# The first five rotations wholly on VectorE, one value tile back between indexer blocks, an earlier sum of squares and odd modulations on VectorE

## What is computed

```
ada = silu(c) @ w_ada + b_ada                     # shifts, scales, gates
h = rms_norm(x, g_pre_mix) * (1 + sc1) + sh1      # modulated input
qa, ka, va, qi, ki, wi, qb, kb, vb, ga, gb = split(h @ w_in)
qa, ka, qi, ki, qb, kb = rope(...)                # rotary positions
score = sum over 8 heads of wi * relu(qi . ki)    # indexer, masked; top-k keys per query
oa = attention(qa, ka, va) over the top-k keys
ob = differential attention(qb, kb, vb)
m = sigmoid(ga) * (oa @ w_o_a) + sigmoid(gb) * (ob @ w_o_b)
x = x + gate * rms_norm(m @ w_out)
x = x + gate * rms_norm(swiglu(modulated rms_norm(x)))
```

## Time and profile before

| | us |
|---|---|
| median of 3 runs (1062.88 to 1063.39) | 1063.2 |
| the profiled execution's own time | 1065.39 |
| its span, first to last instruction | 1063.5 |
| PE busy in the span | 970.6 |
| DVE / ACT / POOL busy | 397.4 / 403.1 / 384.8 |

### The profile page before, as it was taken

One profiled execution on the slowest core, in us unless ns is written; L12 is line 12 of the kernel. 1 busy time (PEld: TensorE's weight loads), 2 busy tenths in 40 slices (PEclk: granted clock), 3 DMA queues, 4 the chain that ended last, 5 costly groups with the idle time before them and its releaser, 6 DMA issues.

```text
span 1063.5 us, 17552 instructions
## 1 busy us (share of the span) xinstructions
PE 970.6 (91%) x7100; PEld 920.0 (87%) x7100; DVE 397.4 (37%) x734; ACT 403.1 (38%) x723; POOL 384.8 (36%) x194
## 2 busy tenths in 40 slices
PE   4789797999999989989999659999999999999995
PEld 1677797999988989878888449999999999999995
DVE  3566884876764333143200552222222221000005
ACT  3654223656555455343333362222222222322221
POOL 2443016466263231224544203333333332444440
PEclk9899898999999999989999889999999999999998
DMA  9631012222222013247865102222222221222212
GB/s 369 251 118 45 1 56 96 99 96 71 102 93 71 21 43 131 72 156 259 319 214 193 39 1 82 87 89 79 79 79 80 90 86 54 83 82 83 82 56 90
DMA packets 33663, 111.58 MB, mean 105 GB/s; under 512 B 4224, under 2 KB 7296, under 8 KB 33216
## 3 DMA queue, kind: packets, MB, share of 16 engines
q1 hardware_dynamic: 29216, 102.48, 27.6%
q10 hardware_dynamic: 4112, 6.93, 1.7%
q0 software_dynamic: 272, 1.31, 0.3%
HBM read 100.38 MB, written 10.32 MB: 104 GB/s over the span
## 4 chain that ended last, share of the span: by engine, by line
PE 77%; issue 8%; ACT 5%; DVE 5%; POOL 2%; DMA 1%; SPq 0%; ACTq 0%; DVEq 0%; POOLq 0%
PE pj L1502 53%; PE pj L1714 12%; PE pvb L1624 3%; PE lg L1474 2%; PE tb L1608 2%; PE pj L1687 1%; DMA raw<-in_w_ada 1%; PE lg L1737 1%; PE lg L1739 1%; PE lg L1738 1%; PE pj L1493 1%; DVE ro L536 1%; ACT hf L961 1%; POOL zc L1056 1%; ACT whi L707 1%
## 5 line engine op out<-in xcount | busy, mean ns | idle before, releaser
L1502 PE MATMUL pj<-hh,whi 128*128 128x288 f32 x1248 | 279.2, 306 | 23.4 <-DVE hl L1189 15.5
L1502 PE MATMUL pj<-hl,whi 128*128 128x288 f32 x1248 | 269.9, 298 | 0.0
L1502 PE MATMUL pj<-hh,wlo 128*128 128x288 f32 x1248 | 269.7, 298 | 0.0
L1502 PEld LDWEIGHTS pj<-hh,whi 128*128 128x128 f32 x1248 | 202.6, 192 | 29.2 <-issue 19.1
L1502 PEld LDWEIGHTS pj<-hl,whi 128*128 128x128 f32 x1248 | 204.0, 192 | 0.0
L1502 PEld LDWEIGHTS pj<-hh,wlo 128*128 128x128 f32 x1248 | 203.5, 191 | 0.0
L1019 POOL TENSOR_TENSOR wlo<-raw,whi 128x1024 fp32r<-128x1024 f32 x53 | 128.5, 2425 | 153.0 <-ACT whi L707 152.5
L1100 POOL TENSOR_TENSOR wlo<-raw,whi 128x1024 fp32r<-128x1024 f32 x41 | 97.9, 2389 | 199.9 <-ACT whi L986 199.9
L1426 DVE TENSOR_TENSOR ft<-pj,sg 128x576 f32<-128x576 f32 x22 | 16.7, 757 | 193.7 <-PE pj L1502 193.7
L1115 POOL TENSOR_TENSOR dlo<-rawd,dhi 128x1408 fp32r<-128x1408 f32 x16 | 51.6, 3223 | 82.7 <-ACT dhi L969 82.7
L986 ACT ACTIVATE whi<-raw 128x1024 fp32r<-128x1024 f32 x41 | 43.3, 1056 | 95.6 <-PE pj L1502 95.6
(11 more groups left out here) (177 smaller groups left out, 1646.8 us busy)
## 6 DMA issues: line engine op xcount, KB each, us to landing
raw<-in_w_s SPq DMA_DIRECT2D x94, 512.0 KB, 3.5
rawa<-in_w_ada SPq DMA_DIRECT2D x32, 512.0 KB, 6.3
rawd<-in_w_d SPq DMA_DIRECT2D x16, 704.0 KB, 4.0
raw<-in_w_ada SPq DMA_DIRECT2D x16, 512.0 KB, 10.4
g_raw<-gz ACTq DMA_DIRECT2D x16, 288.0 KB, 2.1
gate<-g_raw SPq DMA_DIRECT2D x8, 576.0 KB, 3.9
rawv<-in_w_v SPq DMA_DIRECT2D x8, 324.0 KB, 4.8
xt<-in_xT SPq DMA_DIRECT2D x2, 1152.0 KB, 6.9
```

The costliest lines, as they stand in the source:

```text
L1502: ins = mm(pj[tile % 2][:, h, 0:HALF], w[:, slot(c), b:b + P], x[:, kc, h * HALF:(h + 1) * HALF], start=(kc == first and w is whi and x is ...
```

## The change

Four edits. (1) `turns_of` does a whole rotation on one engine; the first five run on VectorE, so GpSimd's `zc` multiply falls away there and GpSimd has only the weight block's low part to make. (2) Value tile 3 is projected behind block 4 of the indexer instead of before it. (3) The sum of squares goes to PE behind the third modulation chunk instead of the fifth, ScalarE loads its table for the root ahead of that, and the first weight block is rounded behind the root. (4) Odd `modulate0` move from GpSimd to VectorE with a new order there, and `first_parts` 1 and 2 move behind `ada_rows(1)`.

```
-        s += [("v", 4), ("v", 3)] if t == 4 else [("v", t)] if t != 3 else []
+        s += [("v", t)]
...
+        def turns_of(eng, c, r):
+            eng.wait_ge(pj_act, taken(tile_of[c], "A"))
+            if r >= 1:
+                eng.wait_ge(rope_o, r)
+            eng.tensor_tensor(zc[:, :], z[:, :], cos[:, :], ALU.mult).then_inc(zc_ready, 1)
             eng.tensor_tensor(zs[:, :], zs[:, :], sin[:, :], ALU.mult).then_inc(zs_ready, 1)
             eng.wait_ge(zs_ready, r + 1)
             eng.wait_ge(zc_ready, r + 1)
...
+            act.activation(scratch[:, 0:1], eps[:, 0:1], ACT.Sqrt)
+            rms(tile_of["stat0"], rms0, 0)
             hi(0)
-            rms(tile_of["stat0"], rms0, 0)
...
-            lo(0)
-            lo(1)
-            modulate0(1)
-            modulate0(3)
-            modulate0(5)
-            modulate0(7)
-            lo(2)
+            for c in range(3):
+                lo(c)
...
-                        pool.wait_ge(pj_act, taken(tile_of[c], "A"))
-                        if r >= 1:
-                            pool.wait_ge(rope_o, r)
-                        pool.tensor_tensor(zc[:, :], z[:, :], cos[:, :], ALU.mult).then_inc(zc_ready, 1)
                         if r >= N_KI:
-                            half_turn(pool)
-                            add_turns(pool, r)
+                            turns_of(pool, c, r)
...
+            def modulate0(kc):
+                v.wait_ge(gs_ready, 2 * (kc // 4 + 1))
+                v.wait_ge(xn_ready, kc + 1)
+                if kc >= 3:
+                    v.wait_ge(h_lo, kc - 2)
+                for w, c0, c1 in SPANS:
+                    ins = v.tensor_scalar(hf0[:, kc % 3, c0:c1], xt[:, kc, c0:c1], gs[:, 0, kc, w:w + 1], ada[:, kc, w:w + 1],
+                                          ALU.mult, ALU.add)
+                ins.then_inc(hf_ready, 1)
+            for half in range(2):
+                if half:
+                    ada_columns(1)
+                    scale0(1)
+                modulate0(4 * half + 1)
+                lo_h0(4 * half)
+                if not half:
+                    normalise(2)
+                    normalise(3)
+                modulate0(4 * half + 3)
+                for kc in range(1, 4):
+                    lo_h0(4 * half + kc)
+                    if not half:
+                        normalise(kc + 3)
+                if not half:
+                    normalise(KC - 1)
...
-                if k == 4:
+                if k == 2:
                     stat(tile_of["stat0"], [acc0], [(acc_ready, KC - 1)])
...
-                if k in (KC + 3, KC + 5, KC + 7):
-                    first_parts((k - KC - 3) // 2)
+                if k == KC + 3:
+                    first_parts(0)
             ada_rows(1)
-            for kc in range(3, KC):
+            for kc in range(1, KC):
                 first_parts(kc)
```

More of the change, by code:

```diff
@@ L521, in slot_free @@
                 wait_used(eng, c - RING)
-        def half_turn(eng):
+        def turns_of(eng, c, r):
[3 more added lines that the diff above has]
+            eng.tensor_tensor(zc[:, :], z[:, :], cos[:, :], ALU.mult).then_inc(zc_ready, 1)
             eng.tensor_tensor(zs[:, :], zs[:, :], sin[:, :], ALU.mult).then_inc(zs_ready, 1)
-        def add_turns(eng, r):
             eng.wait_ge(zs_ready, r + 1)
@@ L1177, in _ @@
             scale0(0)
-            for kc in range(2, 4):
-                normalise(kc)
             def gain_scale(n, sc):
@@ L1218, in rope @@
                 r = ROPE_AT[CH[c]]
-                v.wait_ge(pj_act, taken(tile_of[c], "A"))
-                half_turn(v)
-                add_turns(v, r)
+                turns_of(v, c, r)
             def rope_lo_part(c):
```

## The result

The changed kernel takes 1055.3 us (median of 4 runs, 1051.3 to 1056.54) against 1063.3 (4 runs, 1062.88 to 1063.45): ratio 0.9919, 95% interval 0.9896 to 0.9942. The forecast was 1056.1 with a range of 1047.5 to 1060.5. The profiled execution is the fastest of the four: 1051.3, span 1049.4; the one of the kernel before, 1065.39, was slower than its median. So its trace shows 14.1 us where the medians show 8.0, and the first task is to see which of the 14.1 belong to the change.

A forecast was written before the change was run, and what follows sets the result against it. Bound: PE, busy behind 181 us, before that waiting on the opening's chain, ScalarE's copies in the rotations and VectorE in the indexer. 3.4 + 3.7 + 0.7 - 0.7 = 7.1 us takes 1063.2 to 1056.1, range 1047.5 to 1060.5.

The forecast's parts named there:

- The opening: Up to the first tile's copy-out: copied out at 48.0 against 51.44, 3.4 us gained.
- 15.0, 18.1 and 28.7: In the opening: starts of the root's matmuls, the reciprocal and the first part on PE, in us.
- the collision of the normalising multiplies with GpSimd: In the opening: GpSimd's low part of weight block 1, 21.5 to 23.9, falls on the first normalising multiply.
- the prediction's upper bound: Opening: 4.1 us gained if PE's clock is up already at chunks 12 to 15; ScalarE then ends last.
- PE ends last: End of the opening: PE's parts run to 47.9, ScalarE ends near 47.3, just ahead of PE.
- The rotations: First five rotation rounds: each 0.74 us shorter, together 3.7 us gained.
- E + 4.3: In a rotation round: the add ends 4.3 us after E, the end of the copies, against E + 5.04.
- the rival that the add goes first: Rotations: the add precedes GpSimd's low part, rounds shrink below PE's 6.8 us; gain 16.1, total 1047.1; chance 0.16.
- The 115 ns: Rotations: skill's delay after VectorE's end before the blocked side goes on; by it the add would be just first.
- The value tile: Indexer: block 4 starts 0.7 us earlier; PE idle 5.4 us ahead, low clock costs 1.7, net -0.7 there.
- Rival 3: Indexer: clock stays down into value tile 3 or through tile 2; 1064 or 1070 us; chance 0.08.
- rival 1: Rotations: the add goes first, waits of 7.0 us go, PE sets the pace; total 1047.1 us; chance 0.16.

The follow-up runs named there:

- e11: The changed kernel again, unaltered, measured beside others on one chip against the kernel before: 1054.01 us, ratio 0.9931.
- e9: As e5, but GpSimd's low part starts directly behind the add in rounds 3 and 4, behind block 4's multiply-adds in round 5: 1043.85 us, ratio 0.9815.
- e1: The kernel before with only the opening's edits (earlier sum of squares, odd modulations on VectorE, order of first parts): ratio 0.9963.
- e6: As e5, with value tiles 4 and 3 both ahead of block 4 again: 1053.45 us, ratio 0.9910.
- e2: The kernel before with only the first five rotations wholly on VectorE: ratio 0.9960.
- e4: The kernel before with only value tile 3 moved behind block 4: ratio 1.0000.
- e3: The kernel before with the first five rotations on VectorE and value tile 3 behind block 4: ratio 0.9969.
- e10: The changed kernel with half of value tile 3 ahead of block 4 and half behind it: 1055.43 us, ratio 0.9940.
- e5: The changed kernel with GpSimd's weight-block low part waiting for something of VectorE's in each of five rounds: 1049.51 us, ratio 0.9873.
- e8: The changed kernel with first parts 1 and 2 between the modulation chunks again: 1053.57 us, ratio 0.9914.

## Why the prediction was right

**The opening (3.4 forecast).** The steps hold to 0.3 us up to the first product (15.0, 18.1 and 28.7 forecast; 14.73, 17.83 and 28.68 measured), and so does the collision of the normalising multiplies with GpSimd. Behind it the term was too small in the trace: 6.0 between the two profiled executions. There the clock's low stretch came earlier, while PE works through blocks that arrive slower than it computes anyway; that was the case of the prediction's upper bound and more. In other executions the gain was 5.3 (e11), and in e9 2.4; the means of all traces lie 4.1 apart, and the time of e1 is 3.9 us (1.9 to 5.9), so both lie by the 3.4. "PE ends last" held in e6 and e9 only; in the changed kernel ScalarE's value blocks do.

**The rotations (3.7).** The add at E + 4.3 was E + 4.32, and GpSimd did get in between zs and the add in every one of five rounds (2.84, 2.84, 2.81, 2.83 and 2.78 us): the rival that the add goes first fell. The way from first copy-out to block 4 became 4.6 us shorter, 4.4 forecast with the 0.7 of the value tile; e2 alone gave 4.2 us in time (2.2 to 6.4). The 115 ns that the prediction takes from the Trainium skill (SBUF — State Buffer, "A bandwidth-pool intuition that's wrong") are no guide for who is first here: the add was at most 0.05 us behind zs and still lost.

**The value tile (0.7 - 0.7).** Idle time 4.60 for 5.4, low clock for block 4 as forecast, at 1.95 for 1.7. From block 4 to the first logits the changed kernel takes 1.1 us more than before (79.7 against 78.6) and 2.2 more in e11 (80.8), 0.7 forecast. e4 and the pair e2 and e3: nothing, to within about 2 us. So that the edit nets to nothing by itself is measured as far as that; that the clock lengthens block 4 is shown by e10.

**The sum.** 7.1 forecast, 8.0 measured, with e1 and e2 at 3.9 and 4.2. The mechanism came as forecast; that the total is within 1 us is in part luck. Up to the first logits the two traces of the changed kernel gained 9.5 and 7.7: the opening gave 2.6 and 1.9 more than its term, the way to block 4 0.2 more, and block 4 to the first logits 0.4 and 1.5 less. The profiled execution would have come to 1058.3; it came to 1051.3, and most of that difference is in the opening's clock (2.6) and in the code behind the first logits (4.6), which was not forecast and which no run shows to be the change's. Rival 3 (low clock into value tile 3) did not occur: the clock is up again from 90 us, and the tile takes 7.1 us, from 93.15 to block 3's first matmul at 100.27. What the prediction missed is what it could have read from rival 1: the wait in the port costs a round more (2.1 us in the add) than the engine of the cosine multiply (0.7), and three waits on GpSimd's side bring another 10 us of median (e9 against e11). With the add made to go first, e5 came to 1049.5 and e9 to 1043.9, where rival 1 had 1047.1.

## What to carry to other kernels

Moving an operation from GpSimd to VectorE shortened this chain by 0.7 us a round (the two multiplies end 1.46 us after the copies instead of 2.08), but the next two-input operation still stood behind what GpSimd had started in the meantime; look for that operation (2.8 us where 0.76 is usual) and give GpSimd's work a later trigger, on an event after which VectorE has nothing urgent. An edit that measures as nothing (value tile 3) can be worth 4 us after another one, so try it again once the limit beside it has moved. And one profiled execution can be off by as much as the whole effect: divide it by milestones, and count only what lies in the code that changed.

## What the runs showed of the hardware that was not expected

GpSimd's operation held up a VectorE operation of only eight columns with one input in SBUF: 2.14 us instead of 0.17. A pause of 1.79 us on PE, among other short ones, preceded a low level of TensorE's clock for some 7 us (e9); in the changed kernel's trace the pause at that place was 0.64 us and the clock stayed up. Ahead of block 4 idle times of 4.60 us (changed kernel) and 4.54 us (e8) gave a first matmul of 0.79 and of 0.50 us: the same pause did not bring the clock down at the same moment. Executions of one kernel lay 12 us apart (1053.27 to 1065.38 for the kernel before, beside e9 to e11), and those of e9 14 us.
